# Two more feed-forward pairs by seven products, attention pieces ahead of the last gate unit, and fillers in the last head pair

## The reference

```python
# first block: a mixer (gated convolution beside gated linear attention), then the feed-forward
x = x + rmsnorm(mixer(rmsnorm(x, g1), w_in, ...), g2)
h = rmsnorm(x, g3)
u = dwconv3(h @ w_up, conv_w)            # w_up: 1024 x 5632; convolution of width 3 over tokens
gate, val = split(u)                     # 2816 and 2816 channels
x = x + rmsnorm((silu(gate) * val) @ w_down, g4)
# second block: attention with low-rank queries and keys, 8 heads, one layer
proj = rms_norm(x, l0_norm) @ l0_w_in    # queries' 384, keys' and values' 256, rope 64, gate 1024
q = rms_norm(c_q) @ w_uq;  kv = rms_norm(c_kv) @ w_ukv
o = softmax((q_nope @ k_nope.T + rope(q_pe) @ rope(k_pe).T) * scale) @ v
x = x + (o * silu(gate)) @ l0_w_out
out = rms_norm(x, final_norm)
```

## Time and profile before

| | us |
|---|---|
| median of 3 runs (lowest, highest) | 1787.15 (1786.33, 1787.56) |
| the profiled execution's own time | 1786.32 |
| its span, first to last instruction | 1784.4 |
| PE busy | 1751.6, 98% of the span |
| DVE busy | 1195.2, 67% |
| ACT busy | 771.2, 43% |
| POOL busy | 523.4, 29% |
| mean granted PE clock | 0.997 |

### The profile page before, as it was taken

One profiled execution on the slowest core, in us unless ns is written; L12 is line 12 of the kernel. 1 busy time (PEld: TensorE's weight loads), 2 busy tenths in 40 slices (PEclk: granted clock), 3 DMA queues, 4 the chain that ended last, 5 costly groups with the idle time before them and its releaser, 6 DMA issues.

```text
span 1784.4 us, 21029 instructions
## 1 busy us (share of the span) xinstructions
PE 1751.6 (98%) x8288; PEld 1436.9 (81%) x8288; DVE 1195.2 (67%) x1275; ACT 771.2 (43%) x984; POOL 523.4 (29%) x217
## 2 busy tenths in 40 slices
PE   8999999999999999999999999999999999999997
PEld 5778888887888888888788888787788888888786
DVE  7454677848697978878764674764576767676533
ACT  5332222255333555555432433422256666666522
POOL 3457554454121000000264345054421111211051
PEclk9999999999999999999999999999999999999999
DMA  5223222154311122222364355312301111102232
GB/s 185 112 96 118 78 77 83 37 163 151 123 71 72 59 83 94 72 83 94 130 218 148 118 190 176 130 54 77 107 30 36 36 48 36 47 12 71 89 130 94
DMA packets 59434, 170.79 MB, mean 96 GB/s; under 512 B 7632, under 2 KB 8016, under 8 KB 59344
## 3 DMA queue, kind: packets, MB, share of 16 engines
q1 hardware_dynamic: 41488, 120.67, 20.5%
q10 hardware_dynamic: 17856, 48.87, 7.4%
HBM read 131.24 MB, written 38.27 MB: 95 GB/s over the span
## 4 chain that ended last, share of the span: by engine, by line
PE 88%; DVE 6%; ACT 4%; issue 1%; DMA 1%; POOL 0%; ACTq 0%; DVEq 0%
PE psum L671 22%; PE psum L975 15%; PE psum L988 13%; PE psum L710 7%; PE psum L1099 5%; PE psum L1120 5%; PE psum L1156 5%; PE psum L1051 4%; PE psum L870 3%; PE psum L1109 3%; PE psum L692 1%; PE psum L1076 1%; DVE ptl L2341 1%; ACT pth L1714 1%; PE psum L816 1%
## 5 line engine op out<-in xcount | busy, mean ns | idle before, releaser
L583 POOL TENSOR_TENSOR wl<-wstage,wh 128x1024 fp32r<-128x1024 f32 x101 | 262.1, 2597 | 245.8 <-ACT wh L1246 205.5
L578 POOL TENSOR_TENSOR wh<-wstage,ones 128x1024 fp32r<-128x1024 f32 x52 | 126.0, 2423 | 549.0 <-PE psum L1099 307.4
L671 PE MATMUL psum<-hh,wh 128*128 128x512 f32 x608 | 194.1, 400 | 0.9 <-ACT root L1249 0.9
L671 PE MATMUL psum<-hl,wh 128*128 128x512 f32 x608 | 187.6, 390 | 0.0
L671 PE MATMUL psum<-hh,wl 128*128 128x512 f32 x608 | 187.3, 389 | 0.0
L583 POOL TENSOR_TENSOR wx<-wstage,wx 128x1024 fp32r<-128x1024 f32 x25 | 61.6, 2465 | 378.2 <-ACT wx L1246 378.2
L2099 DVE SCALAR_TENSOR_TENSOR cc<-uu,col,cc 128x1023 f32<-128x1023 f32 x88 | 128.8, 1463 | 49.0 <-ACT cc L1462 47.4
L671 PEld LDWEIGHTS psum<-hh,wh 128*128 128x128 f32 x608 | 112.2, 188 | 29.4 <-issue 6.0
L671 PEld LDWEIGHTS psum<-hl,wh 128*128 128x128 f32 x608 | 114.1, 188 | 24.2
L671 PEld LDWEIGHTS psum<-hh,wl 128*128 128x128 f32 x608 | 114.1, 188 | 24.2
L2341 DVE TENSOR_TENSOR ptl<-psum,pth 128x1024 fp32r<-128x1024 f32 x64 | 78.3, 1224 | 55.4 <-ACT pth L1714 55.4
(11 more groups left out here) (362 smaller groups left out, 4365.0 us busy)
## 6 DMA issues: line engine op xcount, KB each, us to landing
wstage<-w_units SPq DMA_DIRECT2D x161, 512.0 KB, 3.8
acts<-cc ACTq DMA_DIRECT2D x22, 512.0 KB, 2.6
hhf<-acts SPq DMA_DIRECT2D x27, 256.0 KB, 4.2
mix<-spill ACTq DMA_DIRECT2D x12, 512.0 KB, 2.6
resid<-yo SPq DMA_DIRECT2D x24, 256.0 KB, 2.0
hlf<-acts SPq DMA_DIRECT2D x17, 256.0 KB, 4.0
kq<-mix SPq DMA_DIRECT2D x16, 256.0 KB, 4.1
gates<-gspill ACTq DMA_DIRECT2D x8, 512.0 KB, 2.6
```

The source lines that it names most:

```text
L578: pool.tensor_tensor(high, stage(u), ones[:, :].unsqueeze(1).to_broadcast([P, 8, P]), ALU.mult).then_inc(w_high, 1)
L583: pool.tensor_tensor(low, stage(u), high.bitcast(F32), ALU.subtract).then_inc(w_split, 1)
L671: mm = pe.matmul(out[:, t], w[:, wslot, b, :], x[part][:, xk, t], start=start and n == 0, stop=stop and n == 2)
```

## The change

1. `SP` goes from 7 to 5: five plain pairs, 17 pairs by seven products. `LATER` makes all eight `normalised` tiles in the first pair and every later job one pair earlier; T1's and T3's high parts move one pair earlier too. `SW_MADE` counts T2 ahead of T4. At the switch T4's high and low part and the evacuation and centre tap of the last pair's first unit move behind P6, P5, T2 and P7. The places that the down weights wait for are renamed to fit, and the last C12 is taken ahead of the last value taps.
2. In `next_layer` the norm sum of the second half moves from behind the k loop to behind its step 5 (both layers); for n = 1 the norm sum of the first half goes behind the second matmul group, and the other sum from group (0, 1) to (0, 3), with a wait for `h_lo` in front of each group of j = 0.
3. ACT, not POOL, makes the high parts of the attention's units 5 to 13 (`BY_ACT`); the calls stand between its squares, gate tiles and roots.
4. PE makes the four `FIRST` pieces ahead of the last gate unit; gate tiles 6 and 7 go to `sq`, and the last one comes behind the pieces on ACT and DVE. In the first step table the banks alternate from the start (`OPENING`).
5. In the last head pair the heads' loads and splits start in the first head (`LOAD_AT`, `HEAD_AT`), ACT's `head_high` stands ahead of the step's exp, DVE's `head_low` ahead of the reciprocal, and PE makes the first half of output unit 0 in six of the second head's steps (`FILL_AT`), 3 matmuls each, into bank 7. `PART` reorders where the heads lie.

```diff
-SP = 7
+SP = 5
-BY_ACT = (1, 2, 3, *range(U_OUT + 2, U_L0 + 5),)
+BY_ACT = (1, 2, 3, *range(U_OUT + 2, U_L0 + 14),)
-SW_MADE = ("T1", "T3", "B11", "B21", "T4", "T2", "B22")
+SW_MADE = ("T1", "T3", "B11", "B21", "T2", "T4", "B22")
+PART = (3, 4, 0, 1, 2)
...
-                return product_done(FT - 1, ("P5", "P5", "P2", "P5", "P4")[u - U_DOWN])
+                return product_done(FT - 1, ("P5", "P5", "P5", "P4", "P2")[u - U_DOWN])
...
+        OPENING = tuple((at, where, kind, 6 + j % 2) for j, (at, where, kind, _b) in enumerate(PIECES[0]))
+        HEAD_AT = ((0, 6), (0, 7), (1, 3), (1, 4), (1, 5), (1, 6))
+        FILL_AT = ((1, 0), (1, 1), (1, 4), (1, 5), (1, 6), (1, 7))
+        LOAD_AT = ((0, 3), (0, 3), (0, 7), (1, 2), (1, 4), (1, 5), (1, 6))
... next_layer (PE)
-                norm_sum_half(n, 0, sum_bank)
+                if n == 2:
+                    norm_sum_half(n, 0, sum_bank)
...
+                        if n == 1 and j == 0:
+                            pe.wait_ge(h_lo, KT + k + 1)
                         mm = half_products(bank(2 * j), places[j], k, 0, k == 0, k == KT - 1)
+                        if n == 1 and (j, k) == (0, 1):
+                            norm_sum_half(n, 0, sum_bank)
...
-                pe.wait_ge(half_tile, n)
-                norm_sum_half(n, 1, 0)
+                    if k == 5:
+                        pe.wait_ge(half_tile, n)
+                        norm_sum_half(n, 1, 0)
... (PE) the pieces move into the loop over the attention's units
+                if j == len(L0_SLOTS) - 1:
+                    pe.wait_ge(evac, E_LAST - 2)
+                    pe.wait_ge(c_lo, CT)
+                    for number, kind in enumerate(FIRST):
+                        piece(number, kind, *first_banks(number), -1, 1)
... head_pair (PE)
+                        if last and (par, n) in FILL_AT:
+                            k = FILL_AT.index((par, n))
...
+                            pe.wait_ge(ol_ready, k + 1)
+                            last_products(0, k, (0,))
... the switch (ACT)
             right_high("B21", KT)
-            right_high("T4", KT + 4, (sw_lo, made("B11", 1)))
-            old_centre(SP - 1, 0)
             product_high(SP, "P6")
             product_high(SP, "P5")
             right_high("T2", KT + 3, (unit_done, U_SW))
             product_high(SP, "P7")
+            right_high("T4", KT + 4, (sw_lo, made("B11", 1)))
+            old_centre(SP - 1, 0)
             product_high(SP, "P4")
             snap(SP, 0)
... head_pair (ACT)
+                        if last and (par, n) in HEAD_AT:
+                            head_high(HEAD_AT.index((par, n)))
                         exponents(pair, par, n)
... (DVE)
-            LATER = (((0, 1), (2, 3)), ((4, 5), (6, 7)), ("T1", "T3"), ("T2", "T1 low"), ("T4", "T3 low"))
+            LATER = (((0, 1, 2, 3), (4, 5, 6, 7)), ("T1", "T3"), ("T2", "T1 low"), ("T4", "T3 low"))
... the switch (DVE)
             right_low("B21", 0, 1)
-            right_low("T4", 0, 1)
-            projected(SP - 1, 0)
             product_low(SP, "P6")
             product_low(SP, "P5")
             right_low("T2", 0, 1)
             product_low(SP, "P7")
+            right_low("T4", 0, 1)
+            projected(SP - 1, 0)
             product_low(SP, "P4")
... after the last pair (DVE)
             a_low(0)
+            taken_part(FT - 1, "C12")
             taps(FT - 1, 1, 0)
             a_low(1)
-            taken_part(FT - 1, "C12")
```

More of the change, by code:

```diff
@@ L407, in block_kernel, with order_of @@
         PAIR = len(PIECES[0]) + len(PIECES[1])
+        def order_of(pair, par):
+            return OPENING if isinstance(pair, int) and pair == par == 0 else PIECES[par]
         def pieces(pair, par, step, place, last):
             base, found = pair * PAIR + (len(AHEAD) + len(PIECES[0]) * par), []
-            for j, (at, where, kind, bk) in enumerate(PIECES[par]):
+            order = order_of(pair, par)
+            for j, (at, where, kind, bk) in enumerate(order):
                 if (at, where) == (step, place) and not (last and par and kind in AHEAD):
-                    before = max((k + 1 for k in range(j) if PIECES[par][k][3] == bk), default=bk - 7)
+                    before = max((k + 1 for k in range(j) if order[k][3] == bk), default=bk - 7)
                     found.append((base + j, kind, bk, base + before))
@@ L424, in out_of_6 @@
         def out_of_6(pair, par, step):
-            last = max(j for j, p in enumerate(PIECES[par]) if p[0] <= step and p[3] == 6)
+            last = max(j for j, p in enumerate(order_of(pair, par)) if p[0] <= step and p[3] == 6)
             return pair * PAIR + (len(AHEAD) + len(PIECES[0]) * par) + last + 1
@@ L1079, in piece @@
                 mm.then_inc(piece_done, 1)
+            for j in range(5, len(L0_SLOTS)):
+                if j == len(L0_SLOTS) - 1:
[3 more added lines that the diff above has]
+                        piece(number, kind, *first_banks(number), -1, 1)
+                pe.wait_ge(w_split, U_L0 + j + 1)
+                pe.wait_ge(evac, E_L0 + 1 + max(n for n in range(j) if L0_SLOTS[n] == L0_SLOTS[j]))
+                if j == 11:
+                    pe.wait_ge(c_root, 2)
+                unit(slot(L0_SLOTS[j]), ring(U_L0 + j), H)
+                if j in (8, 9):
+                    if j == 8:
+                        pe.wait_ge(evac, E_L0 + 8)
+                    else:
+                        pe.wait_ge(c_root, 1)
+                    pe.wait_ge(cacc_step, (QT, CT)[j - 8])
+                    sums(slot(3), (acc, root)[j - 8][:, :]).then_inc(csum_done, 1)
             def scores(pair, par, n):
@@ L1122, in weigh, with last_products @@
                 mm.then_inc(pv_done, 1)
+            def last_products(m, k, halves=(0, 1)):
+                for n in range(3):
+                    w, part = SPLIT[n]
+                    for half in halves:
+                        t = slice(half * HT, half * HT + HT)
+                        mm = pe.matmul(last_out(m, half), w[:, ring(U_LAST + m), k, :], head_parts(k)[part][:, t],
+                                       start=k == 0 and n == 0, stop=k == KT - 1 and n == 2)
+                return mm
             def head_pair(pair, first, last):
@@ L1148, in _ @@
             head_pair(3, False, True)
-            def last_products(m, k, halves=(0, 1)):
-                for n in range(3):
-                    w, part = SPLIT[n]
-                    for half in halves:
-                        t = slice(half * HT, half * HT + HT)
-                        mm = pe.matmul(slot(m % 3)[:, t], w[:, ring(U_LAST + m), k, :], head_parts(k)[part][:, t],
-                                       start=k == 0 and n == 0, stop=k == KT - 1 and n == 2)
-                return mm
             def first_heads(m, ks):
@@ L1648, in _ @@
             norm_root(2, 1, 0)
+            weight_high(U_L0 + 5)
             act.wait_ge(kp_sum, 1)
@@ L1676, in _ @@
                     gate_tile(2, 2)
-            for m in range(3, KT):
+            weight_high(U_L0 + 13)
+            for m in range(3, KT - 1):
                 gate_tile(m, m % 3)
@@ L1760, in head_pair @@
                                 store_head(*before, 1)
+                            else:
+                                for r in range(2):
+                                    act.wait_ge(gate_out[r], 3 * DMA)
                             fetch_gate(pair, par, 0)
```

97 lines of the change are left out of this document (47 added, 50 removed).

## The result

The changed kernel takes **1790.35 us** (median of 10 runs, 1789.02 to 1793.07) against 1786.86 (10 runs beside it, 1786.05 to 1787.57): ratio 1.0021, 95% interval 1.0013 to 1.0029. The forecast was 1780, range 1772 to 1785: wrong, and in its sign.

What follows compares the result with a forecast made beforehand. PE, busy 98%, was taken as the bound. Savings of 14.2 us against 7.6 lost at the switch gave -6.6 on the profiled 1786.3, so 1779.7; with the median 0.8 above, the forecast was 1780, range 1772 to 1785.

Steps and rivals of the forecast that it cites:

- The 24 matmuls: Two more pairs by seven products, 84 matmuls each instead of 96: 5.4 us less PE work.
- The switch's wait: At the switch P6 waits for ACT's snap, behind DVE's late evacuation of the last plain pair: +6.0 us, bounds nothing to 8 more.
- The low clock there: PE's standstill at the switch drops its granted clock to half: +1.6 us, bounds 0 and 1.9.
- Norms: For n = 1, 6 more matmuls hide PE's wait of 0.8 us for ACT's last squares: -0.9 us.
- Down: C12 ahead of the taps removes a 0.9 us wait, `a_low(1)` adds some 0.5: -0.6 us, bounds -1.1 and +1.
- The projection's root: In the attention's projection, POOL idle beside DVE's three low parts removes PE's 0.9 us wait for the second root: -1.0 us.
- The opening: At the attention's start, early pieces and alternating banks remove waits and low clock, 1.0 us staying at turn 1: -4.8 us.
- The last pair: In the last head pair, fillers bridge two long `ptl` waits while early splits add some wait: -1.5 us, bounds -3 and +1.
- (b): Time freed in the attention returns as later waits at its opening and last head pair: 1784.5 us, chance 0.13.
- Rival (c): DVE's queue at the switch is longer, taps in pairs 1 and 3 also taking 4.62 us: 1787.8 us, chance 0.07.
- Rival (a): The switch costs nothing, DVE reaching B11 early or ACT's snap not waiting: 1772 us, chance 0.20.
- POOL beside DVE: At the switch and down, two taps beside POOL's split take 4.62 instead of 2.60 us, 2.0 more per set.

Runs made afterwards that it cites:

- e9: Changed kernel with both of ACT's snaps at the switch ahead of the last pair's evacuation, snap 1 no longer waiting for it: 1793.06 us, ratio 1.0038.
- e15: Changed kernel with 16 pairs, snaps first, DVE's and ACT's switch work sorted by PE's need, POOL's split later, C12 and `a_low(1)` ahead of taps: 1783.04 us.
- e2: Changed kernel with POOL's split of unit `U_ATT + 3` waiting until DVE has lowered turn 0: 1785.18 us, ratio 0.9996.
- e3: Changed kernel with `a_low(1)` as well as C12 ahead of the value taps, and `a_low(2)` ahead of the gate taps: 1787.52 us, ratio 1.0009.
- e17: Changed kernel with 16 pairs, the unchanged kernel's switch order, POOL's split later, C12 and `a_low(1)` ahead of the taps: 1777.65 us, ratio 0.9957.
- e4: Changed kernel with ACT's snap 0 at the switch moved right behind T2's high part, ahead of the evacuation: 1790.9 us, ratio 1.0027.
- e13: Changed kernel with both snaps first and DVE's and ACT's switch work sorted by when PE needs it: 1790.11 us, ratio 1.0024.

## Why the prediction was wrong

- **The 24 matmuls** (-5.4): right.
- **The switch's wait** (+6.0): mechanism, place, releaser and the order of the queue right, size 7.5 with the refill, from pair 0's tiles. But I charged it as the one price of two pairs more and asked nothing of what came behind P6. e9 to e15 show that P6 was only the first of several products that wanted DVE's work.
- **The low clock there** (+1.6): 2.6 in the profiled execution, 0.5 to 1.9 net. "By the rule the fall is sure" (the Trainium skill, TensorE: Matmul & The Clock Gate, What's actually happening): it fell at every wait of 4 us or more, in every kernel, and, leaving out the last 20 us of a kernel, at none of 1.2 or less. Between them it is open: behind the 2.25 us wait at the down product it fell in after, not in e2 (1.00 throughout), where the first half of down is 1.6 us shorter.
- **Norms** (-0.9): right. From PE's last long stretch ahead of the norm (392.05 and 392.57) to its fifth unit (491.34 and 490.97) it is 0.9 us shorter. The other 1.0 that takes this row of the ledger to +0.1 is 0.5 us lost in small steps ahead of 392 us, 0.2 to 1.5 in the experiments, whose cause is open, and 0.5 between the fifth unit and P1, 0.4 of it a wait for B11's low part.
- **Down** (-0.6, bound +1): **+2.9, failed.** I had seen that `a_low(1)` would stand behind taps that POOL slows, and priced them by the row with 4.62, where one POOL pass lay beside them. Here two did, since C12 made the taps later: 6.29. The 2.3 us wait brought the clock down, which I had not added; in e2, where the clock stayed up, the row is +1.3. e3 shows the repair.
- **The projection's root** (-1.0): right, -1.1, with DVE's pair of numbers.
- **The opening** (-4.8, bounds -5.7 and -3): **+0.3, the step that cost most.** "1.0 us of wait stays" held DVE's chain behind R1 at its old length, and turn 1 waited 4.15. The length hung on POOL's start, which PE releases, and PE was moved: 1.38 us became 4.79. e2 takes the collision away with one wait; the opening then yields 4.6 and the attention 6.5, where 4.8 and 7.3 were forecast.
- **The last pair** (-1.5): -1.1, with one wait of 1.19 at the turn behind the splits, as put.
- **The tail**: +0.9, and not in the forecast: after's last matmuls ran at 1.2 GHz (the clock is 0.52 in 1780 to 1782), before's at 2.4. e2 and e17, which end as after does, take 86.2: it comes and goes from one execution to another.

Of the rivals (b), the freed time comes back as later waits, was the nearest: it had 2.8 us coming back at the opening, and 5.1 did, by a collision that it doesn't name. Rival (c) named the right queue and the wrong reason: taps in pairs 1 and 3 ran at 2.60, pair 2's at 4.62, as counted. Rival (a), that 17 pairs cost nothing at the switch, is refuted by every order tried (after, e4, e9, e13: 6.9 to 10.3 us above clean).

On POOL beside DVE I kept the row against the Trainium skill's rule (SBUF — State Buffer, Who interferes with whom: an exclusive lock, the loser blocked for a whole instruction), because in the row both engines lengthened. That was misread. The traces agree with the rule: the single rows above show each engine waiting for the other's instruction, and both lengthen where each loses in turn. DVE lost 3.4 us at the opening and 3.7 at down, to two POOL passes each time. The price hangs on how many passes are met; my one row carried the price of one.

## What to carry to other kernels

Replacing work on the bounding engine by work on a second one is worth its matmuls only if the second has a gap where it comes due; add up that engine's queue not to the first consumer, but until it has caught up, and look for what can go into its gaps before shortening its lead. When a stage is moved, find each engine that it releases (here POOL, by PE's count) and what stands beside it at its new time: a collision that the old trace only just missed is a coming one. A wait for an engine with nothing urgent can be the cheapest edit of all.

## What the hardware showed

- Two DVE instructions of 32x512 with both inputs in SBUF took 1.38 us alone and 4.79 beside two of POOL's passes over 128x1024; two 128x1023 taps 2.60 alone, 4.62 beside one pass, 6.29 beside two. Each blocked one ended a fixed time after POOL's pass, 0.54 and 1.08 us, so the small ones lengthen most in proportion.
- What reads PSUM on DVE was not longer beside POOL: in before `ptl<-psum,pth` took its 1.22 at 1308.18, inside POOL's pass from 1307.46.
- Behind the same 7.3 us wait the granted clock stayed low for 10.2 us in after and for 6.8 in e2 and e3. In all three it had fallen while PE stood still, so a long wait hides part of its own low clock.
- Eight float32 matmuls of no use, run inside that wait, kept the clock at 2.4 GHz, did not delay P6, and brought nothing that the median shows.
